# Local outputs computed turned, retention units of two heads, and a unit's steps placed apart

## The reference

```python
# branch 1: 8 query heads over 2 key heads of 64 wide, sink s per head
p = softmax(concat([s, q @ kc.T, where(|i - j| <= 128, q @ k.T, -inf)]) )[1:]
o = p_ctx @ vc + p_win @ v
# branch 2, 4 heads, both directions: position decay gamma**|i - j|
o = ((q @ k.T) * decay) @ v        # then group norm per head, times silu(gate)
# branch 0: two maps per head
a = softmax(q1 @ k1.T) - lam * softmax(q2 @ k2.T);  o = a @ v
y = sum_b sigmoid(gate_b) * (o_b @ w_branch[b]);  x = x + g1 * (y @ w_out)
```

## Time and profile before

| | |
|---|---|
| median of 3 runs | 1891.33 us (1888.51 to 1893.94) |
| profiled execution | 1888.46 us, span 1886.8 us |
| TensorE products | 1671.3 us busy, 89% of the span |
| weight loads (beside the products) | 1047.2 us, 56% |
| VectorE | 479.3 us, 25% |
| ScalarE | 324.8 us, 17% |
| mean granted clock of TensorE | 0.958 |
| read from memory | 361.37 MB, 200 GB/s over the span |

### The profile page before, as it was taken

How to read it: one execution, slowest core, us unless ns; L and a number is a source line. 1 busy time by engine, 2 the same in 40 slices (tenths; PEclk the granted TensorE clock), 3 DMA queues, 4 the chain that set the end, 5 groups by cost and what they waited for, 6 DMA issues and landing times.

```text
span 1886.8 us, 18860 instructions
## 1 busy us (share of the span) xinstructions
PE 1671.3 (89%) x7425; PEld 1047.2 (56%) x7425; DVE 479.3 (25%) x1093; ACT 324.8 (17%) x705; POOL 74.2 (4%) x97
## 2 busy tenths in 40 slices
PE   4999999999999998799999975999999994777773
PEld 1575657644444466466656643875777883444441
DVE  1222374223232124111111114335333223000002
ACT  3111143212111001000000004124222101000001
POOL 0000000000000000200000000000000001000000
PEclk7999999999999999899999997999999997999997
DMA  9354311043243453588988866321123445899995
GB/s 377 127 201 145 122 56 35 24 156 140 95 142 136 166 203 125 209 335 333 341 316 337 334 232 220 103 77 46 34 90 101 155 158 201 341 404 404 397 395 226
DMA packets 127769, 379.11 MB, mean 201 GB/s; under 512 B 8531, under 2 KB 84461, under 8 KB 113117
## 3 DMA queue, kind: packets, MB, share of 16 engines
q1 hardware_dynamic: 118208, 354.44, 50.6%
q0 software_dynamic: 6688, 18.93, 3.2%
q10 hardware_dynamic: 2812, 4.91, 0.7%
HBM read 361.37 MB, written 16.88 MB: 200 GB/s over the span
## 4 chain that ended last, share of the span: by engine, by line
PE 76%; DMA 14%; DVE 4%; ACT 3%; issue 2%; POOL 1%; ACTq 0%; POOLq 0%; SPq 0%; DVEq 0%
PE ps L764 19%; PE ps L962 13%; PE ps L831 11%; DMA ring<-in_w_exp_gate 9%; PE ps L834 8%; PE ps L977 6%; PE ps L1127 6%; PE ps L1084 3%; PE ps L777 2%; PE ps L867 1%; PE ps L862 1%; DMA residual<-in_x 1%; PE ps L857 1%; DMA arena<-moe_rows,idx_i 1%; PE ps L885 1%
## 5 line engine op out<-in xcount | busy, mean ns | idle before, releaser
L764 PE MATMUL ps<-ring,arena 128*128 128x256 f32 (+1 forms) x1152 | 308.7, 428 | 2.7 <-DVE arena L1739 1.5
L962 PE MATMUL ps<-hT,ring 128*128 128x512 f32 (+1 forms) x768 | 263.4, 492 | 10.3 <-ACT arena L1356 8.1
L764 PEld LDWEIGHTS ps<-ring,arena 128*128 128x128 f32 x1152 | 219.1, 191 | 96.3 <-issue 70.9
L831 PE MATMUL ps<-hT,ring 128*128 128x512 f32 (+1 forms) x544 | 211.6, 543 | 3.2 <-ACT arena L1307 2.3
L962 PEld LDWEIGHTS ps<-hT,ring 128*128 128x128 f32 x768 | 142.1, 190 | 124.0 <-issue 113.9
L834 PE MATMUL ps<-ring,hT 128*128 128x256 f32 (+1 forms) x832 | 173.1, 366 | 5.8 <-DVE arena L1591 3.1
L834 PEld LDWEIGHTS ps<-ring,hT 128*128 128x128 f32 x832 | 147.0, 190 | 36.9 <-issue 19.9
L1084 PE MATMUL ps<-ring,arena 128*64 128x256 f32 x1024 | 129.1, 411 | 40.3 <-DMA ring<-in_w_exp_gate 22.7
L831 PEld LDWEIGHTS ps<-hT,ring 128*128 128x128 f32 x544 | 102.4, 193 | 102.7 <-issue 96.8
L977 PE MATMUL ps<-arena,ring 128*128 128x512 f32 (+1 forms) x384 | 133.8, 488 | 1.7 <-DVE arena L1739 1.0
L1084 PEld LDWEIGHTS ps<-ring,arena 128*64 128x64 f32 x1024 | 78.4, 148 | 97.2 <-DMA ring<-in_w_exp_gate 32.2
(11 more groups left out here) (206 smaller groups left out, 1189.1 us busy)
## 6 DMA issues: line engine op xcount, KB each, us to landing
ring<-in_w_exp_gate SPq DMA_DIRECT2D x32, 2048.0 KB, 9.7
ring<-in_w_exp_up SPq DMA_DIRECT2D x32, 2048.0 KB, 10.3
ring<-in_w_exp_down SPq DMA_DIRECT2D x32, 2048.0 KB, 10.9
ring<-in_w_in SPq DMA_DIRECT2D x54, 1024.0 KB, 6.0
ring<-in_w_ada SPq DMA_DIRECT2D x48, 1024.0 KB, 7.1
ring<-in_w_branch SPq DMA_DIRECT2D x24, 512.0 KB, 3.5
ring<-in_w_out SPq DMA_DIRECT2D x8, 1024.0 KB, 6.7
moe_results<-arena SPq DMA_DIRECT2D x16, 512.0 KB, 10.1
```

Source lines behind the costliest of these rows:

```text
L764: last = pe.matmul(dst, a, b, start=(i == 0), stop=(i == len(pairs) - 1))
L831: last = pe.matmul(ps[:, n % 2, 0:tok.stop - tok.start], w[:, k, at:at + width], hT[:, k, tok], start=(k == 0), stop=(k == KD - 1))
L962: last = pe.matmul(ps[:, 0, lo:TOK], kview(n)[:, k, P * (m % 2):P * (m % 2 + 1)], hT[:, k, lo:TOK], start=(k == 0), stop=(k == KD - 1))
```

## The change

- Local outputs: the product has V (64 columns) as the stationary operand and the turned probabilities as the moving one, so it gives the turned output; head j = 0 goes to output partitions 0 to 63, j = 1 to 64 to 127, alternating over the key tiles. VectorE divides the probabilities ahead of their transposition, and copies the output times 0.5 straight to `oT[1]`. `turn_o(1, j)`, its copies and the gates' waits for them go. `oT[0]` and `oT[1]` trade places.
- Retention units hold two heads and one query tile. The numbers of units, masks and output products stay; the scores are products of 128 columns in the two row halves alternately.
- The plan has steps: the exponentials of unit n stand 1.7 us of stream behind the unit's entry, the divisions (kind "b") and the combination of the two maps (kind "a") 3.8 us, squares and norms behind those. TensorE turns unit n-1 behind `divided` for both kinds.
- Late parameters are issued by SP behind the ninth weight tile, the retention exponents first and the constants last. Their use (`cols`: transposition, copy, exponentials, VectorE's constants) stands behind the first projection tile's two jobs.
- `ctx` has a semaphore of its own, and ScalarE waits for each half of the tokens as it comes to it.

```diff
         probT = region(17920, 1024)
-        o_tok = [chunks(0, NT, BW), chunks(20992, NT, BW), chunks(18944, NT, BW)]
+        o_tok = [chunks(0, NT, BW), None, chunks(18944, NT, BW)]
...
-        oT = [chunks(20992, KB), chunks(12288, KB), chunks(2048, KB)]
+        oT = [chunks(12288, KB), chunks(20992, KB), chunks(2048, KB)]
...
             q0 = first_tile(l)
-            c = [("c", h, s) for s in ((0, XT) if l < DEPTH - 1 else (XT,)) for h in range(RT_H)]
+            c = [("c", h, t) for t in range(q0, NT) for h in range(RT_H // 2)]
...
-            kind = units[l][i][0]
-            eng.wait_ge({"c": c_masked, "b": b_probs, "a": a_exps}[kind], of_kind(l, i, kind))
+            c = units[l][i][0] == "c"
+            eng.wait_ge(c_masked if c else exps_ready, of_kind(l, i, "c" if c else "ab"))
...
                 mine = [i for i, j in enumerate(jobs[l]) if j[0] == wt]
+                if (l, n) == (0, 1):
+                    add(0.1, "cols")
...
                             add(0, "modulation", l + 1, j // KD)
-                    if b_n == 0 and m >= KB:
-                        add(0.45, "turn_o", 1, m - KB)
...
             after[nc + nb + na + 1] += [("roots", 0)] + [("norm", 0, t) for t in range(first_tile(l), NT)]
-            plan, n = [], 0
+            steps = []
+            for n, t in enumerate(when):
+                end = when[n + 1] if n + 1 < len(when) else t + 9
+                steps.append((t, ("unit", n)))
+                if n < nc + nb + na:
+                    steps += [(min(t + 1.7, end), ("exps", n)), (min(t + 3.8, end), ("divide", n))]
+                steps += [(min(t + 3.8, end), entry) for entry in after.get(n, [])]
+            plan = []
             for entry, t in stream:
-                while n < len(when) and when[n] <= t:
-                    plan.append(("unit", n))
-                    plan += after.get(n, [])
-                    n += 1
+                while steps and steps[0][0] <= t:
+                    plan.append(steps.pop(0)[1])
                 plan.append(entry)
-            return plan
+            return plan + [entry for _, entry in steps]
...
+            def late_params():
...
+
+                sp.dma_start(ret_c, ret_consts.rearrange("p (a u) -> p a u", a=4)).then_inc(ret_in, 16)
+                at = 0
+                for src in (diff_subln_g, ret_gn_g.rearrange("l (k c) -> (l k) c", c=P)):
+                    sp.dma_start(rows_in[at:at + src.shape[0], 1, :], src).then_inc(param_in, 16)
+                    at += src.shape[0]
+                for dst, src in ((loggam[:, :], ret_decay.rearrange("l f h -> (l f h)")),
+                                 (lam_in, diff_lambda.rearrange("l a d -> (l a d)")),
+                                 (sink[:, :], swa_sink.rearrange("l h -> (l h)")), (rbias[:, :], router_b)):
+                    sp.dma_start(dst, src.partition_broadcast(P)).then_inc(param_in, 16)
+                sp.dma_start(rw, router_w.rearrange("(k p) e -> p k e", p=P)).then_inc(param_in, 16)
+                load_bias(sp, 0, 1, 2, bias_in[1])
+                sp.dma_start(cst[:, P:C_END], consts[:, P:C_END]).then_inc(const_in, 16)
...
-
-                sp.wait_ge(oT_ready, 12 * (l + 1))
+                    if n == DIRECT + 1:
+                        late_params()
+
+                sp.wait_ge(oT_ready, 2 * KB * (l + 1))
...
                 pe.wait_ge(h_dve, KD * (l + 1))
-                if l == 0:
-                    pe.wait_ge(param_in, 16 * PARAMS)
-                    pe.transpose(ps[:, 6, 0:NCOL], rows_in[0:NCOL, 1, :], ident[0:NCOL, 0:NCOL]).then_inc(cols_turned, 1)
...
-                        r = slice(HD * (h % 2), HD * (h % 2) + HD)
-                        kts = range(0, XT) if t == 0 else range(0, NT)
-                        q = cqT[r, h // 2, P * t:P * t + 2 * P]
-                        for kt in kts:
-                            last = pe.matmul(pair[:, kt // 2, 2 * P * (kt % 2):2 * P * (kt % 2 + 1)],
-                                             ckT[r, h // 2, P * kt:P * (kt + 1)], q, start=True, stop=True)
+                        for kt in range(keys(units[l][i]) // P):
+                            for j in range(2):
+                                r = slice(HD * j, HD * (j + 1))
+                                last = pe.matmul(pair[:, j, P * (kt ^ 1):P * ((kt ^ 1) + 1)], ckT[r, h, P * kt:P * (kt + 1)],
+                                                 cqT[r, h, P * t:P * (t + 1)], start=True, stop=True)
...
                     if kind == "b":
-                        pe.wait_ge(b_probs, of_kind(l, i, "b"))
+                        pe.wait_ge(divided, of_kind(l, i, "ab"))
...
                     else:
-                        pe.wait_ge(a_comb, of_kind(l, i, "a"))
+                        pe.wait_ge(divided, of_kind(l, i, "ab"))
...
                         pe.wait_ge(c_masked, of_kind(l, i, "c"))
-                        for q in range(2):
-                            last = product(bank[:, P * q:P * (q + 1)],
-                                           [(prob[:, g % 2, 256 * kt + P * q:256 * kt + P * (q + 1)],
-                                             cv[:, kt, P * h:P * (h + 1)]) for kt in range(nk)])
+                        for j in range(2):
+                            last = product(bank[:, P * j:P * (j + 1)],
+                                           [(prob[:, g % 2, 512 * j + P * (kt ^ 1):512 * j + P * ((kt ^ 1) + 1)],
+                                             cv[:, kt, P * (2 * h + j):P * (2 * h + j + 1)]) for kt in range(nk)])
...
                         if kind == "b":
-                            for j in range(2):
-                                kv = (2 * h + j) // (SW_H // SW_KV)
-                                last = product(bank[:, HD * j:HD * (j + 1)],
-                                               [(probT[:, 512 * j + P * k:512 * j + P * (k + 1)],
-                                                 bv[:, k, HD * kv:HD * (kv + 1)]) for k in range(nk)])
+                            kv = 2 * h // (SW_H // SW_KV)
+                            for k in range(nk):
+                                for j in range(2):
+                                    last = pe.matmul(bank[HD * j:HD * (j + 1), 0:P], bv[:, k, HD * kv:HD * (kv + 1)],
+                                                     probT[:, 512 * j + P * k:512 * j + P * (k + 1)],
+                                                     start=(k == 0), stop=(k == nk - 1))
...
                 def unit(n):
+                    if (l, n) == (0, 2):
+                        pe.wait_ge(cols_kept, 1)
...
                         bank = n % 2
-                    elif b == 1:
-                        pe.wait_ge(sig_ready, GB * l + KB + j + 1)
-                        pe.wait_ge(o_kept, base + sum(u[0] != "a" for u in units[l]))
-                        bank = 0
...
                             pe.wait_ge(sig_ready, v)
-                        if b_n == 0 and m > KB or (b_n, m) == (1, 0):
-                            pe.wait_ge(oT_ready, 12 * l + 4 + (m - KB if b_n == 0 else KB))
...
                             arrived(pe, n)
-                        if m == 0:
-                            pe.wait_ge(oT_ready, 12 * l + 4 * b_n + 4)
+                        if m == 0 and b_n == 1:
+                            pe.wait_ge(o_kept, base + sum(u[0] != "a" for u in units[l]))
+                        elif m == 0:
+                            pe.wait_ge(oT_ready, 2 * KB * l + KB * (1 + b_n // 2))
...
-                if l == 0:
-                    pe.wait_ge(cols_kept, 1)
...
                         job(*at)
+                    elif what == "cols":
+                        pe.wait_ge(param_in, 16 * PARAMS)
+                        pe.transpose(ps[:, 6, 0:NCOL], rows_in[0:NCOL, 1, :], ident[0:NCOL, 0:NCOL]).then_inc(cols_turned, 1)
...
                         tile_done(l - 1, t - first_tile(l - 1))
+                    elif t in (0, XT):
+                        act.wait_ge(x_in if t else ctx_in, 16)
...
                         act.activation(xn[:, t, :], res[:, t, :], ACT.Copy, scale=rstd[:, t:t + 1]).then_inc(xn_ready, 1)
-                if l == 0:
-                    late_params()
...
-
-                if l == 0:
-                    act.wait_ge(cols_turned, 2)
-                    act.activation(p_col[:, :], ps[:, 6, 0:NCOL], ACT.Copy).then_inc(cols_kept, 1)
-
-                    act.wait_ge(lam_ready, 1)
-                    act.activation(lam[:, 4:8], lam[:, 0:4], ACT.Exp).then_inc(lam_exp, 1)
-                    act.activation(lgwork[:, 1, :], lgwork[:, 0, :], ACT.Exp).then_inc(lam_exp, 1)
...
                         keep_turned(n - 1)
-                    if n < n_units[l]:
-                        exps(n)
...
                 def keep_o(b, j):
-                    b_n = BRANCH_ORDER.index(b)
-                    act.wait_ge(o_turned, 12 * l + 4 * b_n + j + 1)
-                    bank = {2: banked[l].index(("turn_o", j)) % 2, 1: 0, 0: 2 + j}[b]
```

(52 more changed lines are left out.)

45 lines of the change are left out of this document (15 added, 30 removed).

## The result

The changed kernel takes 1846.51 us (median of 4 runs, 1843.54 to 1849.02), the kernel before 1891.99 (4 runs, 1888.51 to 1893.94). The ratio is 0.9764, 95% interval 0.9743 to 0.9785: about 45 us less, where 44.5 were forecast. The profiled execution took 1843.54 us with a span of 1841.9. An interval of the ratio is some 4 us either way.

A forecast was written before the change was run, and what follows sets the result against it. TensorE was taken to bound the mixers, and the first projection's start the stretch ahead of them. Terms 9.7 + 12.3 + 12.6 + 8.6 + 1.3 = 44.5 us off the 1891.33 median gave 1847 us, range 1837 to 1867.

The forecast's parts named there:

- The start: Ahead of the mixers: separate ctx semaphore and late loads on SP start the projections at 41.4, 9.7 us earlier (7 to 10.5).
- six of the eight pairs of hT copies: At the start, before the first projection: two pairs of copies at 0.57 us, six at 0.82.
- The transposes: Retention gates: 24 transposes go with their copies and 8.1 us of gate waits; 12.3 us saved (4.2 to 12.3).
- The turned local product: Local outputs: column halves run in pairs, 1.06 us a latent unit and 0.63 a context unit; 12.6 us saved.
- The rival that the halves pay their loads: Local products: each pass pays its load, 1.92 and 1.06 us a unit, 4.6 us lost; 1864 us, chance 0.06.
- Retention scores: Retention units: 128-column passes in alternating row halves, 1.06 us for 1.92 latent, 0.63 for 1.06 context; 8.6 us saved.
- Modulation: TensorE's 3.0 us wait ahead of a modulation tile: merge now goes first, about 1.3 us go (0 to 2).
- VectorE and the small waits: Mixers: added divisions hide; up to 6 us lost at squares set against up to 6 of small waits gone, counted nothing.
- TensorE busy without a gap from 216 on, no wait on the divisions: Expected sign in the mixers; a wait over 1 us on VectorE's divisions ahead of turns would show it wrong.
- the rival (the squares ahead of the next maxima): Mixers: squares behind the division delay the next maxima, 12.6 us in all, some 9 if partly hidden; 1856 us, chance 0.08.
- the cover of a latent unit: Between exponentials' end and next turn in latent local units: 1.1 to 1.6 us remain after sum, reciprocal and division.

The follow-up runs named there:

- divide_earlier: Changed kernel with only the division moved to 2.6 us of stream behind the unit instead of 3.8; median within 1848 to 1856 us.
- transposes_back: Changed kernel with four groups of transposes a layer, ScalarE's copies and the gates' waits for them put back among the retention gates; median 1853.19 us.
- steps_together: Changed kernel with exponentials, division and branch squares, roots and norms all directly at the unit's entry; median 29 us longer than the changed kernel.
- local_in_order: Changed kernel with the turned local product doing all key tiles of head 0, then head 1; mixer stretches 7.3 us longer.
- ret_in_order: Changed kernel with retention scores doing all key tiles of the first head, then the second; ratio 0.9775 to the kernel before.
- both_nearer: Changed kernel with exponentials 0.8 and division 3.0 us of stream behind the unit, squares at 3.8; its stretches are 2.7 us longer.
- ctx_joint: Changed kernel with ScalarE waiting for ctx and x together before the first square; first projection at 42.6 us, median 1844.46 us.
- ctx_joint_act: Changed kernel with ctx and x awaited together and the eleven late loads issued by ScalarE behind the normalisations; first projection at 50.1 us against 39.4.
- params_on_act: Changed kernel with the eleven late parameter loads issued by ScalarE behind its last xn; first projection at 41.2 us against 39.4.

## Why the prediction was right

The forecast was 1847 with a gain of 44.5 us. The time is 1846.51, and the start and the four mixer stretches gained 47.4. That the median hits to half a microsecond is partly luck: these stretches gained 3 us more than forecast, and the experts, which the forecast left as they were, took 2.5 us longer in the profile. The terms:

- **The start, 9.7 forecast, 11.7 measured,** and 1.3 more behind it, since the first 64 passes and the modulation tile behind them no longer begin at the lower clock (29.9 us for 31.15 at a granted clock of 1.00 for 0.95). The steps came as written: ctx's squares at 17.09, hT from 34.74 with no issue ahead of it, the parameters landed when wanted. The step that was mis-sized is six of the eight pairs of hT copies, taken at 0.82 us a pair as before; at the clock's upper level they take about 0.54 (six copies of ScalarE in 3.25 us), and the projections start at 39.35 instead of 41.4. That is partly luck: divide_earlier, whose edit lies elsewhere, started at 40.8 with a clock of 0.50 between 35 and 39 us. The forecast has both halves in one chain and doesn't ask what one alone gives; either alone gives most of it (9.9 and 8.5 of the 11.7 us, with the late use of the parameters in all).
- **The transposes, 12.3 forecast:** 9.6 are theirs by transposes_back, and the other 2.7 of the waits counted had another cause, most likely what stood ahead of the copy on ScalarE. They went too, so the sum holds.
- **The turned local product, 12.6 forecast:** 1.02 us instead of the forecast's 1.06 for a latent group and 0.59 instead of 0.63 for a context one. Against 1.73 and 0.84 in the trace of before (the forecast took 0.86) that is 16 x 0.71 + 8 x 0.25 = 13.4. Reading the pair's rate from the experts of layer 1 was the right row. The rival that the halves pay their loads is refuted: it had 1.92 us, and 16 loads and 16 passes take 1.02, with all 128 rows in both halves. With it the rule of the Trainium skill (TensorE: Matmul & The Clock Gate, Part 3, The mechanism) that a load overlaps only where the row group differs does not hold for this product.
- **Retention scores, 8.6 forecast:** 8 x 0.82 + 4 x 0.41 = 8.2.
- **Modulation, 1.3 forecast:** the pause went from 3.02 to 1.66, 1.4 us. It does hang on the place of the steps: it is 3.88 in steps_together. Not counted was the granted clock behind it, 0.50 in before for 3.4 us and 1.00 in the changed kernel: the tile's 8 passes took 1.93 us and take 1.06, 0.9 more.
- **VectorE and the small waits, counted at nothing, 6 either way.** They do come to about nothing, but from parts of 8 to 9 us that cancel, which is luck. Against the change: the divisions are late in five places, all in layer 0, which costs 7.2 us and, behind the longest, some 1.7 of lower clock. For it: in layer 1 four more waits among the gates (0.5 to 1.0 us, 2.7 in all) and one of 2.27 us at a rotation's job copy have gone, for a new one of 0.93; in layer 0 two waits for job copies, 1.58 and 0.46 us, have gone; and before had 3.4 us at the lower clock behind its 2.27, some 1.7 us, where layer 1's mixer is now at 1.00 throughout. That is 8.9 against 7.8. The two pieces at the lower clock in before, the first at the pause of 3.02 us (under Modulation) and the second behind that of 2.27:

```profile
484.50:487.90 3.40, 3.07 (x10) 0.92 (x11) 0.23 (x2) 0.00 (x0) 0.00 (x0) 0.50 0.00 0
1276.40:1279.80 3.40, 3.40 (x10) 2.68 (x9) 1.32 (x4) 0.81 (x3) 0.00 (x0) 0.50 0.00 0
```

The step of this last term that was wrong is the wait it had at nothing: "TensorE busy without a gap from 216 on, no wait on the divisions". The mechanism named for the rival (the squares ahead of the next maxima) is a part of it, and the trace has the rest. VectorE and ScalarE of the changed kernel, ahead of the longest wait:

```profile
224.15 0.68 DVE L1696 TENSOR_REDUCE mnh<-arena 128x4 f32<-128x512 f32 x1
...
228.76 0.16 DVE L1623 TENSOR_SCALAR st<-st 128x2 f32<-128x2 f32 x1
232.27 0.43 DVE L1564 TENSOR_TENSOR arena<-arena,cst 128x256 f32<-128x256 f32 x1 [3.34 <-ACT arena L1300]
...
233.80 0.62 DVE L1641 TENSOR_SCALAR arena<-arena,st 128x256 f32<-128x256 f32 x2
...
228.96 0.47 ACT L1314 ACTIVATE arena<-ps,st 128x256 f32<-128x256 f32 x1 [3.53 <-DVE st L1623]
...
230.10 1.53 ACT L1299 ACTIVATE arena<-ps 32x256 f32<-32x256 f32 x4
...
234.56 0.63 PE L914 MATMUL ps<-cst,arena 128*128 128x128 f32 x4 [2.99 <-DVE arena L1641]
```

The squares make the maxima late (they end at 228.9), so the exponentials end at 230.1. ScalarE's job copy stands behind these, until 232.2. VectorE's rotation of that job stands ahead of the division, which could have run at 230.1 and runs at 233.4. The forecast looked at the cover of a latent unit (over 1 us left) and at the squares' 3.2 us, but not at what stands between exponentials and division on both queues.

All terms together, as measured, are 11.7 + 1.3 + 12.3 + 13.4 + 8.2 + 1.4 + 0.9 - 1.1 = 48.1, where the stretches have 47.4.

**What was not foreseen at all** is how much the placement carries. The divisions add 19 us to VectorE (18 forecast); the forecast let them hide if they were ready in time, and set what the places of the steps cost and give against each other at nothing. With the steps together TensorE has the same passes, and two thirds of the gain are gone. Before, with its own order, had less of this loss: its exponentials stood at the unit's entry too, but in the local units no division stood ahead of the turn, since the output was scaled instead. So the placement seems less a gain of its own than what keeps the division that the turned product needs from costing as much as it gains. That is a reading: no run places the steps of the old product apart.

## What to carry to other kernels

Cut traces at the same instructions and compare stretch by stretch: a mixer stretch repeated to 0.1 us (but for 1.7 us of lower clock in two profiles) where the median of five runs was known to 4 either way. When work is moved to an engine that is half idle, its place in the queue is worth more than its duration: put the step that waits for another engine behind the copy that a third one needs, and look at what stands between the two halves of a chain on every queue it passes. Where the clock falls behind a wait, the wait costs more than its length: read the busy time of the stretch as well as the waits. Where two changes remove the same obstacle, try each alone before crediting both.

## What the runs showed of the hardware

Passes on two halves of the array's columns or rows run together even when they are not neighbours in the list: heads in order, with eight passes each, overlapped from the fifth on (1.51 us instead of 1.02, and no loss at four passes each). That was on halves of the columns; on halves of the rows the group's time and the starts say the same (1.64 for 1.10). A pass of 128 columns that ran alone took 0.109 us, and so did a pair. The same section of the Trainium skill (TensorE: Matmul & The Clock Gate, Part 3, The mechanism) says that matmuls start and end strictly in program order. In local_in_order and ret_in_order the starts don't fit that, by the times above and if the pass with the longer record is the second head's first, as it is read here.

The granted clock fell to 0.50 in or behind a pause of TensorE of 2.99 us in the changed kernel, of 3.02 and 2.27 in before, and of 2.67 to 4.80 in steps_together, where passes that took longer made up 11 of the 33 us. The length of the pause alone doesn't decide it: behind a pause of 2.27 us both_nearer stayed at 1.00, and behind the same pause of 1.83 us ctx_joint fell and the changed kernel didn't.

One and the same pair of bias-row issues held its queue for 5.0, 5.2, 5.8 and 7.4 us in four kernels. The time at which it stands is not all of it: in before and in ctx_joint_act it began at 36.3 and 36.5 us and took 5.8 and 7.4; what differs is the order of the other loads, of which ctx_joint_act has the retention constants in front. The issue of these held SP for 10.9 us in the changed kernel and ScalarE for 0.35 in params_on_act. The cause stays open. An issue's length is read where it will stand, not where it was.
